# Layer 0's two attentions with the turns of the probabilities one step later

## The reference, cut to what matters

```
qa, ka, va, qb, kb, vb = split_cols(h @ w_in, EVEN_SPLITS)
qa, ka = rms_norm(qa, g0), rms_norm(ka, g1); rope on x's q and k
a:  p = softmax(q @ k.T);  o = p @ v                       # 8 heads of 64
b:  p = softmax(q @ k.T)  for two heads j = 0, 1 of a pair
    a = p[0] - lam * p[1]; o = a @ v                       # 4 pairs, v of 128
o_b = rms_norm(o_b, subln_g) * (1 - lam0)
out = concat(o_a, o_b) @ w_out
```

## Time and profile before

| what | value |
|---|---|
| median of three runs | 1560.24 us (1560.18 to 1560.88) |
| profiled execution, own time | 1565.27 us |
| its span, first to last instruction | 1563.5 us |
| mean granted TensorE clock | 0.991 |
| PE busy | 1523.6 us (97%) |
| DVE busy | 866.1 us (55%) |
| ACT busy | 676.4 us (43%) |
| POOL busy | 167.5 us (11%) |

### The profile page before, as it was taken

The page is one execution under the profiler, slowest core; times in us unless marked ns, Lnnn a source line. Parts: engine busy times, 40 slices in busy tenths (PEclk is TensorE's granted clock), DMA queues, the critical chain, the costliest instruction groups (busy, mean ns, idle before and its releaser), DMA issues.

```text
span 1563.5 us, 24063 instructions
## 1 busy us (share of the span) xinstructions
PE 1523.6 (97%) x9482; PEld 1290.6 (83%) x9482; DVE 866.1 (55%) x1497; ACT 676.4 (43%) x1089; POOL 167.5 (11%) x165
## 2 busy tenths in 40 slices
PE   9999999999999988999999999999999999999998
PEld 7998798999997865786789777777787887779987
DVE  6786654544545874427775343433448646665544
ACT  5454344545444444425655122222224546644443
POOL 2200310000000110001214001110011020011010
PEclk9999999999999988999999999999999999999999
DMA  6456655453436314311222453534422421145451
GB/s 251 184 208 217 242 216 186 161 192 136 162 135 243 131 61 179 146 54 54 82 101 89 161 192 131 215 150 174 188 81 92 146 75 54 69 175 216 178 199 55
DMA packets 43769, 233.80 MB, mean 150 GB/s; under 512 B 13264, under 2 KB 14224, under 8 KB 16784
## 3 DMA queue, kind: packets, MB, share of 16 engines
q1 hardware_dynamic: 31232, 222.38, 38.4%
q10 hardware_dynamic: 12432, 9.94, 2.2%
HBM read 231.22 MB, written 1.08 MB: 149 GB/s over the span
## 4 chain that ended last, share of the span: by engine, by line
PE 86%; DVE 8%; ACT 2%; issue 2%; POOL 1%; DMA 1%; SPq 0%; DVEq 0%; ACTq 0%
PE ps L553 24%; PE ps L555 23%; PE ps L554 23%; PE ps L770 5%; PE ps L742 3%; PE ps L656 3%; PE ps L708 2%; DVE wlo L1079 2%; PE ps L700 2%; POOL flo L2425 1%; ACT whi L1069 1%; PE ps L640 1%; DMA raw<-in_wstream 1%; DVE nmax L1885 1%; PE ps L950 1%
## 5 line engine op out<-in xcount | busy, mean ns | idle before, releaser
L1079 DVE TENSOR_TENSOR wlo<-raw,whi 128x2048 fp32r<-128x2048 f32 x162 | 381.9, 2380 | 241.7 <-ACT whi L1069 241.4
L1069 ACT ACTIVATE whi<-raw 128x2048 fp32r<-128x2048 f32 x162 | 305.2, 1906 | 213.9 <-PE ps L555 162.9
L553 PE MATMUL ps<-fhi,whi 128*128 128x256 f32 (+1 forms) x1216 | 371.7, 306 | 4.0 <-DVE wlo L1079 1.5
L555 PE MATMUL ps<-fhi,wlo 128*128 128x256 f32 (+1 forms) x1216 | 367.9, 303 | 0.0
L554 PE MATMUL ps<-flo,whi 128*128 128x256 f32 (+1 forms) x1216 | 367.8, 302 | 0.0
L553 PEld LDWEIGHTS ps<-fhi,whi 128*128 128x128 f32 x1216 | 232.1, 191 | 27.6 <-issue 10.4
L555 PEld LDWEIGHTS ps<-fhi,wlo 128*128 128x128 f32 x1216 | 232.2, 191 | 8.9
L554 PEld LDWEIGHTS ps<-flo,whi 128*128 128x128 f32 x1216 | 232.3, 191 | 8.7
L553 PE MATMUL ps<-whi,fhi 128*128 128x512 f32 (+1 forms) x624 | 220.6, 354 | 7.3 <-DVE sumh L2094 4.5
L555 PE MATMUL ps<-whi,flo 128*128 128x512 f32 (+1 forms) x624 | 216.5, 347 | 0.0
L554 PE MATMUL ps<-wlo,fhi 128*128 128x512 f32 (+1 forms) x624 | 216.2, 346 | 0.0
(11 more groups left out here) (263 smaller groups left out, 1814.1 us busy)
## 6 DMA issues: line engine op xcount, KB each, us to landing
raw<-in_wstream SPq DMA_DIRECT2D x210, 1024.0 KB, 5.1
gates<-gated ACTq DMA_DIRECT2D x6, 512.0 KB, 4.4
hx<-in_x SPq DMA_DIRECT2D x1, 1024.0 KB, 5.2
lnrow<-in_ln_g ACTq DMA_DIRECT2D x2, 512.0 KB, 4.3
lnrow<-in_ln_b ACTq DMA_DIRECT2D x2, 512.0 KB, 5.4
hc<-in_ctx ACTq DMA_DIRECT2D x1, 1024.0 KB, 5.4
mix<-in_rpb_rows ACTq DMA_DIRECT2D x4, 256.0 KB, 4.3
hc<-in_rpb_rows ACTq DMA_DIRECT2D x4, 256.0 KB, 3.9
```

Source lines behind the costliest of these rows:

```text
L553: mm(o, lh, rh, start=start, stop=False)
L555: return mm(o, ll, rh, start=False, stop=stop)
L1069: nc.scalar.activation(whi[:, w % SPLIT_SLOTS, :], raw[:, c % RAW_SLOTS, :], ACT.Copy).then_inc(*did("scalar", ("hi", w)))
L1079: nc.vector.tensor_tensor(wlo[:, w % SPLIT_SLOTS, :], raw[:, c % RAW_SLOTS, :], whi[:, w % SPLIT_SLOTS, :].bitcast(F32), ALU.subtract).the ...
```

## The change

Both attentions of layer 0 turn item i-3 at step i, and multiply with the values of item i-4; DVE's outputs come at the item plus 5. The exponentials get four places (the fourth in A is the free half of place 2, in B the scratch tile, which becomes `spare`), and wait for the turn of item i-4. In B every head's maximum raises a semaphore of its own, and each exponential waits for its own. Squares and guess of a pair tile come one step later, and the four squares share one 128-wide scratch, each waiting for the one before. The `ahead` chunk moves from step 2 to step 5. `mod_row` at an even step comes ahead of the maxima, at an odd one right behind them. The turns of the context's heads move into the projection of query tile 1, after 4 and 5 of its 8 k-steps. All other attentions keep their distance of two.

```diff
+        def turned_behind(items):
+            return 3 if items[0][0] in "AB" else 2
+
+        def exp_place(it, i):
+            if it[0] == "A":
+                return e2[:, 2, ETILE // 2:] if i % 4 == 3 else e2[:, i % 4, 0:ETILE // 2]
+            if it[0] == "B":
+                return spare[:, 0:ETILE] if i % 4 == 3 else e2[:, i % 4, :]
+            return (e1 if it[0] == "first" else EE[it[1]])[:, i % 3, :]
...
-                    (2, ("ahead", PLACE[UNIT["q2", 0, 1].w0] + 1)),
+                    (5, ("ahead", PLACE[UNIT["q2", 0, 1].w0] + 1)),
... (PE)
-                    if 0 <= i - 2 < len(items):
-                        turns(i - 2, items[i - 2])
-                    if 0 <= i - 3 < len(items):
-                        values(i - 3, items[i - 3])
+                    if 0 <= i - lag < len(items):
+                        turns(i - lag, items[i - lag])
+                    if 0 <= i - lag - 1 < len(items):
+                        values(i - lag - 1, items[i - lag - 1])
...
-                        turn_heads("q", 0, (2, 3), 4)
-                        turn_heads("k", 0, (2, 3), 2)
-                        by_token(UNIT["q2", 0, 0], ("q2", 0, 0), [1], first=False)
+                        by_token(UNIT["q2", 0, 0], ("q2", 0, 0), [1], first=False,
+                                 between=[(4, lambda: turn_heads("q", 0, (2, 3), 4)), (5, lambda: turn_heads("k", 0, (2, 3), 2))])
... (ACT, exps)
-                    if i >= 3:
-                        act.wait_ge(*after("t", items[i - 3], 0))
+                    if i >= 4:
+                        act.wait_ge(*after("t", items[i - 4], 0))
                     for j, n in parts:
+                        act.wait_ge(*after("max", it, j))
... (ACT, pair_squares and attend)
+                    act.wait_ge(counts.sems["scalar"], counts.now["scalar"])
-                    if 0 <= i - 4 < len(items) and items[i - 4][0] == "B" and items[i - 4][2] == 3:
+                    if 0 <= i - 5 < len(items) and items[i - 5][0] == "B" and items[i - 5][2] == 3:
... (DVE, attend)
+                    if i % 2 == 0:
+                        for m in mods_at(i - 1, items, mods):
+                            mod_row(*m)
                     if i < len(items):
                         maxima(i, items[i])
+                    if i % 2:
+                        for m in mods_at(i - 1, items, mods):
+                            mod_row(*m)
...
-                    if 0 <= i - 4 < len(items):
-                        outputs(i - 4, items[i - 4])
+                    lag = turned_behind(items) + 2
+                    if 0 <= i - lag < len(items):
+                        outputs(i - lag, items[i - lag])
...
-                    if 0 <= i - 5 < len(items) and items[i - 5][0] == "B" and items[i - 5][2] == 3:
-                        pair_norm(items[i - 5][3])
+                    if 0 <= i - 6 < len(items) and items[i - 6][0] == "B" and items[i - 6][2] == 3:
+                        pair_norm(items[i - 6][3])
```

More of the change, by code:

```diff
@@ L363, in build @@
         pair_tmp = tile(att, "pair_tmp", [P, 2, 8])
-        subtmp = tile(att, "subtmp", [P, NW])
-        tile(att, "behind_first", [P, 752])
+        spare = tile(att, "spare", [P, NW + 752])
         ropeg = tile(att, "ropeg", [P, 2, 2, 2, DH])
@@ L736, in turns @@
                 _, kt, _ = item_info(it)
-                e = e1 if it[0] == "first" else EE[it[1]]
+                e = exp_place(it, i)
                 pe.wait_ge(*after("probs", it))
@@ L741, in turns @@
                     for j in range(b, min(kt, b + 4)):
-                        ins = nc.tensor.transpose(o[:, (j - b) * P:(j - b + 1) * P], e[:, i % 3, j * P:j * P + P], ident[:, :])
+                        ins = nc.tensor.transpose(o[:, (j - b) * P:(j - b + 1) * P], e[:, j * P:j * P + P], ident[:, :])
                     ins.then_inc(*did("tensor", ("t", it, b)))
@@ L773, in attend @@
             def attend(items, mods, steps=()):
-                for i in range(len(items) + 3):
+                lag = turned_behind(items)
+                for i in range(len(items) + lag + 1):
                     ahead = 1 if items[0][0] == "B" else 2
@@ L1220, in exps @@
                 parts, kt, _ = item_info(it)
-                e = e1 if kind == "first" else EE[l]
-                act.wait_ge(*after("max", it))
+                e = exp_place(it, i)
+                if kind not in "AB":
+                    act.wait_ge(*after("max", it))
                 if kind in "AB":
-                    if i >= 3:
-                        act.wait_ge(*after("t", items[i - 3], 0))
+                    if i >= 4:
+                        act.wait_ge(*after("t", items[i - 4], 0))
                     for j, n in parts:
+                        act.wait_ge(*after("max", it, j))
                         labels = [("read", "s", it, j)]
@@ L1232, in exps @@
                                 labels.append(("probs", it))
-                        copy(e[:, i % 3, j * 512:j * 512 + n], src("s", it, j)[:, 0:n], ACT.Exp,
+                        copy(e[:, j * 512:j * 512 + n], src("s", it, j)[:, 0:n], ACT.Exp,
                              bias=nmax[:, i % ITEMS_KEPT, j:j + 1], accum_out=rsum[:, i % ITEMS_KEPT, j:j + 1]).then_inc(*did("scalar", *labels))
@@ L1239, in exps @@
                         *did("scalar", ("esink", it)))
-                copy(e[:, i % 3, 0:n], e[:, i % 3, 0:n], ACT.Exp, bias=nmax[:, i % ITEMS_KEPT, 0:1],
+                copy(e[:, 0:n], e[:, 0:n], ACT.Exp, bias=nmax[:, i % ITEMS_KEPT, 0:1],
                      accum_out=rsum[:, i % ITEMS_KEPT, 0:1]).then_inc(*did("scalar", ("exp", it), ("probs", it)))
@@ L1300, in pair_squares @@
                 for h in range(4):
-                    copy(subtmp[:, h * P:(h + 1) * P], mix[:, t, NW + h * P:NW + (h + 1) * P], ACT.Square,
+                    act.wait_ge(counts.sems["scalar"], counts.now["scalar"])
+                    copy(spare[:, ETILE:ETILE + P], mix[:, t, NW + h * P:NW + (h + 1) * P], ACT.Square,
                          accum_out=hss[:, 0, t % 2 * 4 + h:t % 2 * 4 + h + 1]).then_inc(*did("scalar", *([("pair squares", t)] if h == 3 else [])))
             def attend(items, steps=()):
-                for i in range(len(items) + 4):
+                lag = turned_behind(items)
+                for i in range(len(items) + lag + 3):
                     copies_first = items[0][0] in "AB" or (items[0][0] == "C" and i >= 16)
-                    if copies_first and 0 <= i - 2 < len(items):
-                        prob_copy(i - 2, items[i - 2])
+                    if copies_first and 0 <= i - lag < len(items):
+                        prob_copy(i - lag, items[i - lag])
                     if i < len(items):
@@ L1333, in attend @@
                         prob_copy(i - 2, items[i - 2])
-                    if 0 <= i - 4 < len(items) and items[i - 4][0] == "B" and items[i - 4][2] == 3:
-                        pair_squares(items[i - 4][3])
+                    if 0 <= i - 5 < len(items) and items[i - 5][0] == "B" and items[i - 5][2] == 3:
+                        pair_squares(items[i - 5][3])
                     for at, step in steps:
@@ L1884, in maxima @@
                     for j, n in parts:
-                        ins = v.reduce_max(nmax[:, i % ITEMS_KEPT, j:j + 1], src("s", it, j)[:, 0:n], AX_X, negate=True)
-                    ins.then_inc(*did("vector", ("max", it)))
+                        v.reduce_max(nmax[:, i % ITEMS_KEPT, j:j + 1], src("s", it, j)[:, 0:n], AX_X, negate=True).then_inc(
+                            *did("vector", ("max", it, j)))
                     return
@@ L1891, in maxima @@
                     dve.wait_ge(*after("t", items[i - 3], (kb - 1) // 4 * 4))
-                e = (e1 if kind == "first" else EE[l])[:, i % 3, :]
+                e = exp_place(it, i)
                 if kind == "first":
@@ L1981, in attend @@
             def attend(items, mods, steps=()):
-                for i in range(len(items) + 5):
+                for i in range(len(items) + 7):
+                    if i % 2 == 0:
+                        for m in mods_at(i - 1, items, mods):
+                            mod_row(*m)
                     if i < len(items):
                         maxima(i, items[i])
+                    if i % 2:
+                        for m in mods_at(i - 1, items, mods):
+                            mod_row(*m)
                     if items[0][0] == "B" and 0 <= i - 1 < len(items):
                         combine(i - 1, items[i - 1])
-                    if 0 <= i - 4 < len(items):
-                        outputs(i - 4, items[i - 4])
+                    lag = turned_behind(items) + 2
+                    if 0 <= i - lag < len(items):
+                        outputs(i - lag, items[i - lag])
                     for at, step in steps:
```

6 lines of the change are left out of this document (2 added, 4 removed).

## The result

| | changed | before |
|---|---|---|
| median | 1565.88 us (20 executions, 1562.42 to 1570.35) | 1560.78 us (20, 1558.01 to 1565.69) |
| ratio | 1.0035, 95% interval 1.0026 to 1.0044 | |
| profiled execution, span, clock | 1564.04 us, 1562.2 us, 0.992 | 1565.27 us, 1563.5 us, 0.991 |

The account below looks back on a forecast made before the run. PE's own work bounds the kernel; only its idle or low-clock time can be won. A (first attention and what lies ahead) -8.1 plus B (second attention) +4.9 gives -3.2: profiled 1562.1, median 1557.0 us, range 1550.5 to 1563.8.

Parts of the forecast that it names:

- A2: First attention: moving the chunk's low half brings maximum 4 5.2 us sooner, partly given back; with the heads' turns 5.6 kept.
- A1: Ahead of the first attention: context heads turned inside the projection fill PE's 2.7 us wait; first maximum 3.0 us sooner.
- A4: First attention: the third slow-clock stretch, 10.2 us, shrinks to 6.7, a gain of 1.7 us (bounds 0 and -5.1).
- A3: First attention: modulation rows ahead of the maxima at even steps remove PE's waits for sum and row, 0.8 us.
- B1: Second attention: DVE's pace stays 2.57 us a step; DVE is some 1.2 us earlier at step 13.
- B2: End of second attention: POOL a step later starts `fo` 1.2 us later, wait 3.1; extra turn and product add 1.3.
- B3: Second attention's tail: ACT's later squares, each waiting for the one before, delay the last copies, +1.1 us (bounds 0 and 1.9).
- B4: Second attention's tail: the clock falls behind the new 3.1 us wait, +1.3 us (bounds 0 and 5.1).
- R1: Rival, faster: slow stretches go, first attention gains 11.5 us, net -6.6 to -7.9, median about 1553; chance 0.28.
- R2: Rival, no change: banks, not distance, set the first attention, which gains 3.0 + 0.8; net +1.1, 1561.3 us; chance 0.19.
- R3: Rival, slower: each new wait, in both attentions, brings a 10.2 us slow-clock stretch; net +4.0, 1564.2 us; chance 0.18.

Follow-up runs that it names:

- e1: The kernel before, nothing edited, with a second profile: median 1560.07 us, ratio 0.9998; profiled 1561.17 us.
- e8: Changed kernel with the four squares of a pair tile in separate places, without waits among them: median 1564.12 us, ratio 1.0025 to the kernel before.
- e11: Second sample of the kernel before with only the first attention's changes: median 1559.59 us, ratio 0.9991; profiled 1563.54 us.
- e5: Kernel before with only the context heads' turns moved inside the projection of query tile 1: median 1557.90 us, ratio 0.9982.
- e10: The kernel before, nothing edited, with a third profile: median 1560.06 us, ratio 0.9996; profiled 1564.66 us.
- e9: Kernel before with only the heads' turns inside the projection and modulation rows ahead of the maxima: median 1557.62 us, ratio 0.9982.
- e2: Kernel before with all of the first attention's changes, second attention as before: median 1560.44 us, ratio 0.9998.
- e6: Kernel before with the first attention's changes except distance three (turns stay two steps behind): median 1557.68 us, ratio 0.9984.
- e12: Second sample of the first attention's changes at distance two, second attention as before: median 1557.58 us, ratio 0.9986 to the kernel before.
- e7: Kernel before with the first attention's changes except the ahead chunk, which stays at step 2: median 1559.21 us, ratio 0.9985.
- e4: Changed kernel with the four `fo` turns one step later, at steps 17 and 18: median 1560.04 us, ratio 1.0005 to the kernel before.
- e3: Kernel before with only the second attention's changes, first attention as before: median 1565.28 us, ratio 1.0037.

## Why the prediction was wrong

Two steps failed in A, which came out at -2.0 and not -8.1. That is 6.1 of the 7.4 us between the forecast (-3.2) and the sum of what the profiles show (+4.2, below); the rest is in B.

**The larger is A2's second half**, what was to be given back of maximum 4's gain: A1 and A2 together were to leave 5.6 us at scores 12 and 13, and left 1.0 (against e1). The clock fell twice there and not once.

**The other is the base:** "the median of the runs shown is 1560.24, 5.0 us less. I carry the difference over." The difference was no constant. Both profiled executions of before of the longer kind have the third stretch, 10.2 us at half clock, 5.1 us, and the one of the shorter kind lacks it; 19 of 125 executions took the longer time. Terms that take time off this stretch, or off the second one, are worth their price in such an execution and little at the median. A4 (1.7) is such a term: at the median it is 0, and e8 and e11 show that the change doesn't remove the stretch where it does come. The 7.53 us between the two first profiles' marks look like the forecast's 8.1 for A, and that is luck: 5.56 of them lie between two executions of the kernel before itself.

**A, forecast -8.1.** Read against the profile of before that has no third stretch (e1), point by point:
- *A1 right.* Maximum 0 came at 568.80 (forecast 568.6), 3.2 us earlier than e1's 572.04 and 2.8 earlier than in the earlier trace rows. At the median e5 gives 2.7. The stretch behind the wait that it removes is no fixed price either: e10 has the wait and not the stretch.
- *A2, first half right.* Maximum 4 at 576.93 (576.7), 5.4 ahead of e1's 582.37. The wait ends at 575.24 (575.1), though it is 1.9 and not 2.7 us long, and the modulation stands at 575.80 (575.5). The clock falls there, as put. But the wait takes the place of one of 1.73 us, which ACT's high half of the moved chunk had made and which the forecast did not count (PE's waits of the kernel before in A sum to 11.1 us, not 7.5), and the second stretch of the earlier trace rows stood behind that one.
- *A2, second half wrong.* Turn 5 had to come at 585.5 and scores 12 and 13 at 594.5; they came at 586.51 and 598.09, 1.0 us ahead of e1's 599.10. Of the 5.4 us, 4.4 went back between maximum 4 and scores 12. Two stretches of this part lost 1.2 (of 576.9 to 579.3) and 2.9 (half of the 5.81 that PE worked in 586.4 to 592.6), in e1 only 0.7 were lost behind maximum 4 (of 582.4 to 583.8): 3.4 of the 4.4. The other 1.0 is what is left; I put it on waits. I had let the clock fall once, behind the first new wait, and had given PE full speed behind the second one, which I had named. Its 1.8 us are followed by 6.2 us at 0.50; in e11 by 9.9. In e8 the clock does not fall behind the first wait, and turn 5 comes at 585.38, 1.1 us sooner though that execution's A begins 0.54 later (maximum 0 at 569.34): 1.7 us, what a stretch of 3.4 us at half clock costs.
- *A3 right in kind.* The waits on modsum are gone, and from scores 12 to the mark another 1.0 us was won (0.8 forecast). At the median it can't be told from 0 (e9 against e5).

So A measures -2.0 in this profile, -1.2 and -1.3 in e2 and e11, and about -0.9 as the mean of the two ratios (0.9998 and 0.9991). A1 alone is 2.7 at the median, so the rest of A costs time. Distance three is on the losing side: from the first maximum to the mark 75.5 us with it (changed kernel and e2) against 74.0 without (e6 and e12), with equal time at the lower clock. The times point the same way, the three ratios with it (e2, e7, e11) average 0.9991, the three without (e6, e9, e12) 0.9984, which is 1.1 us and less than the half width of any one of their intervals.

**B, forecast +4.9, measured +6.15.**
- *B1 right.* DVE stays at 2.57 us a step, without a gap.
- *B2 right.* A wait of 3.09 us (3.1), POOL's tile 3 late by one step; `fo` 103.04 behind A's mark instead of 101.40: +1.64 (1.2).
- *B2's extra turn and product right, B3 nearly nothing.* From `fo` to the projection 9.88 instead of 5.37, +4.51. Of it 2.9 is half clock (next point), and 1.6 is left for the extra turn and product (1.3 forecast) and B3 (1.1 forecast); PE's only wait there is 0.20 for a copy. e8 puts nothing of it on the squares' own waits; with `fo` a step later (e4) all of it is gone.
- *B4 mis-sized.* 1.3 was put on the clock. The stretch at 0.50 began 0.89 us before `fo`, inside the wait, and PE worked in it from 747.39 to 753.2, 5.8 us: 2.9 lost, and 2.8 in e3's profile. The 2.8 us behind the wait in the earlier trace rows were taken as its likely length; those behind other waits in the same rows were 6.7 and 10.2.

By the rule on transposes in the Trainium skill, page "TensorE: Matmul & The Clock Gate", section "Part 4: PE-mode transpose", B's many transposes would bring the clock down or keep it there. e4 runs the same transposes behind a wait of 1.75 us at a granted clock of 1.00 throughout; so transposes alone don't bring it down here, and the rule's way is not seen. (B's tail opens with 12 transposes, the 8 of `fo` at 753.28 and the 4 at 754.18, and not with 16.)

**The sum.** A at -2.0 and B at +6.2 give +4.2 against e1's execution. Kind against kind the executions give +4.0 and +3.4. The medians' 5.1 holds about one more, which fits where the changed kernel's median falls between its two kinds. Whether the change makes the longer kind more frequent is open: 9 of 20 against 7 of 20 beside it, and 19 of 125 over all.

**The rivals.** R1 did not come. R2 (banks set A) was nearer than the forecast: A kept less than the head start of DVE; its mechanism was not tested, and half clock took most of the rest (3.4 of 4.4 us). R3 had the sign and the mechanism, and its 1564.2 is the nearest. Its sizes were off: 6.7 us instead of 10.2 in B, 3.4 instead of 10.2 behind the wait in A. It had a chance of 0.18; with the base taken right (A4 at 0), the forecast itself would have come out at -1.5. The lower end of the range has a slip: -9.7 is not what R1's own terms give, which with 8.2 for A2 are 8.2 + 0.8 + 5.1 less 4.9 or 3.6, so -9.2 or -10.5.

## What to carry to other kernels

Profile the kernel before twice before a stretch at the lower clock is booked as a gain: if its execution is 5 us off the median, find what makes the 5 us, don't carry them over. An edit that gives a full PE one longer wait can pay more than the wait: the 3.09 us in B were followed by half clock in all three profiles that have them. A shift of a start, here that of the first maximum, is told from what follows it by measuring from that start to the mark. When items are delayed by a step, delay what reads their results by a step too (here `fo`).

## What the runs showed of the hardware

The granted clock of one program differs between executions at the same waits: of three profiles of the kernel before, the stretch behind 600 us came in two, the one behind the wait of 2.7 us near 559 us in two as well, but not the same two, and the one behind 580 us was 3.4, 6.2 or 6.7 us long. The Trainium skill, page "TensorE: Matmul & The Clock Gate", section "Part 1: The HAM clock gate (the "warmup" mystery)", says that the number of slow matmuls at a kernel's start varies between runs of the same kernel; here that holds in the middle of a kernel, and is worth 5.1 us. In B a wait of 3.09 us was followed by 3.4 to 6.7 us at 0.50 in three kernels, and waits of 1.75 (e4) and 0.17 us by none. In A waits of 1.9 us were followed by a stretch in four profiles (changed kernel, e2, e4, e11) and by none in e8, and the 10.1 us in e12 stand behind no wait above 1.0 us: length alone doesn't decide, and what does was not found.
